# Turning the expert product as one tile and three, with the next rows' second half between them

## The chip, the cores and the metric

The kernel runs on one core of a Trainium2 chip. A core has TensorE (matmuls and transposes, PE in the profile, its weight loads PEld), VectorE (DVE), ScalarE (ACT), GpSimd (POOL), SyncE (SP) and DMA queues. The metric is the time of one execution on the device in microseconds (us); it is given as the median of several runs.

## What is computed

One inference step of a decoder trunk with one layer, on 1088 tokens (1024 of a prompt, 64 of samples) of width 1024, in float32. After the mixer come a router and a mixture of 16 experts, of which each token takes two. The change lies in the experts:

```python
hid = jax.nn.silu(jnp.einsum('nd,edf->nef', x, w_gate)) * jnp.einsum('nd,edf->nef', x, w_up)
hid = hid * combine[..., None].astype(hid.dtype)
y = jnp.einsum('nef,efd->nd', hid, w_down)
```

with d = 1024, f = 512 and e = 16 experts. A final RMSNorm follows.

## The kernel before

Five stages run one after another: input projection, attention, output projection with routing, experts, final norm. In the expert stage (`experts`, from L1752) the tokens of each expert are gathered into blocks of up to 128 rows. With these inputs there are 24 blocks for 16 experts: eight experts have one block, eight have two.

Every matmul is done in a split form: an operand is a rounded part (`_hi`) and a remainder (`_rest` or `_lo`), and three products are summed: hi x hi, hi x rest, lo x hi. ScalarE makes each `_hi` by a copy, VectorE each remainder by a subtraction. For the weights these are L1743 and L1748, each on half a matrix (128x2048) at a time, six of each for an expert; the split of the next expert's gate and up matrices is done during the first block of the present expert, that of its own down matrix at the start of that block. So a first block carries twelve of these long instructions on ScalarE and VectorE, and a second block none.

The order on each engine is written out by hand, and semaphores tie them together. For block b:

- TensorE: `project` gate (24 matmuls, L1972, L1973, L1976), then up; four transposes of the next block's rows (`turn_rows(0)`, L1964); four transposes of the product `hid` (L1997), two into `hturn[0]` and two into `hturn[1]`, each pair behind a wait for its part of `hid`; four more of the next rows (`turn_rows(1)`); then the down projection: 16 matmuls with `hidT_hi` as the loaded operand (L2006, L2007), tile by tile, of which tiles 0 and 2 wait for the copy of their pair, and 8 with `hidT_lo` (L2011).
- ScalarE: split of down and gate, `silu` of gate (L1890), splits, then the two copies `hidT_hi` (L1897), the two of the next rows `rowsT_hi` (L1878), a split, and half of `y_out` (L1906), which waits for this block's down projection and for the scatter of the block before to have landed.
- VectorE: splits, the product `hid` of up and silu in two parts (L1937), `hidT_lo` in two parts (L1940), each behind its copy on ScalarE, the next rows' `rowsT_lo` (L1924), splits, the other half of `y_out` (L1951), and the copy of gathered rows into `rows` (L1919).
- GpSimd: the scatter that adds `y_out` to the result (L1864) and the gather of the rows of block b + 3 (L1847). 
- SyncE: loads of the next weights, behind the end of an expert's gate, up and down products.

Of the kernel before, what the change touches and what calls it, by code (L numbers as in the profile page):

```python
# [20 lines left out]
F32 = mybir.dt.float32  # L21
# [4 lines left out]
ALU = mybir.AluOpType  # L26
# [3 lines left out]
P = 128  # L30
# [29 lines left out]
FT = FF // P  # L60
# [1691 lines left out]
def experts(nc, io, keep):  # L1752
# [5 lines left out]
    with ExitStack() as stack:  # L1758
        p = Pools(nc, stack)
# [39 lines left out]
        add_begun = p.sem("add_begun")  # L1799
        expert_begun = p.sem("expert_begun")  # L1800

        def expert_loops(eng, block_step):

            def one(pair, half, last):
                e = 2 * pair + half if pair is not FIRST or half else FIRST
                here = (pair, half)
                following = None if last else ((pair, 1) if half == 0 else (pair + 1, 0))
                first = eng.value_load(ends[0:1, bass.ds(e, 1)], min_val=0, max_val=MAXB - 1)
                after = eng.value_load(ends[0:1, bass.ds(e + 1, 1)], min_val=1, max_val=MAXB)
                block_step(FIRST if e is FIRST else first, here, following)  # L1810
                with eng.If(first + 1 < after):
                    with eng.Fori(first + 1, after) as b:
                        block_step(b)

            one(0, 0, False)
            one(0, 1, False)
            with eng.Fori(1, NE // 2 - 1) as pair:
                one(pair, 0, False)
                one(pair, 1, False)
            one(NE // 2 - 1, 0, False)  # L1820
            one(NE // 2 - 1, 1, True)
# [52 lines left out]
        @block.scalar  # L1874
        def _(act):
            def rows_hi(b, c):
                act.wait_ge(turned, 2 * b + c + 1)
                nc.scalar.activation(rowsT_hi[:, 4 * c:4 * c + 4, :], turn[c][:, :].rearrange("p (k c) -> p k c", k=4), ACT.Copy).then_inc(rowsT_hi_made, 1)  # L1878

            def block_step(b, here=None, following=None):  # L1880

                if here:
                    if b is not FIRST:
                        act.wait_ge(downed, b)
                    moe.split_hi(act, "down", *here, 0)
                    moe.split_hi(act, "down", *here, 1)
                if following:
                    moe.split_hi(act, "gate", *following, 0)
                act.wait_ge(gated, b + 1)
                nc.scalar.activation(silu[:, :], gate[:, :], ACT.Silu).then_inc(silued, 1)  # L1890
                if following:
                    moe.split_hi(act, "gate", *following, 1)
                    moe.split_hi(act, "up", *following, 0)

                for c in range(2):
                    act.wait_ge(hid_turned, 2 * b + c + 1)
                    nc.scalar.activation(hidT_hi[:, 2 * c:2 * c + 2, :], hturn[c][:, 0:2 * P].rearrange("p (k c) -> p k c", k=2),  # L1897
                                         ACT.Copy).then_inc(hidT_hi_made, 1)
                rows_hi(b + 1, 0)
                rows_hi(b + 1, 1)  # L1900
                if following:
                    moe.split_hi(act, "up", *following, 1)
                act.wait_ge(downed, b + 1)
                if b is not FIRST:
                    act.wait_ge(y_stored, 16 * b)
                nc.scalar.activation(y_out[:, 0:512], y[0][:, :], ACT.Copy, scale=slot_w[:, bass.ds(b, 1)]).then_inc(y_act, 1)  # L1906

            rows_hi(FIRST, 0)
            rows_hi(FIRST, 1)
            expert_loops(act, block_step)  # L1910

        @block.vector
        def _(dve):
            def fetch(b):

                if b is not FIRST:
                    dve.wait_ge(turned, 2 * b)
                dve.wait_ge(gathered, 16 * b + 16)
                nc.vector.tensor_copy(rows[:, :], landing[:, :]).then_inc(rows_ready, 1)  # L1919

            def rows_lo(b, c):
                dve.wait_ge(rowsT_hi_made, 2 * b + c + 1)
                hi = rowsT_hi[:, 4 * c:4 * c + 4, :]
                nc.vector.tensor_tensor(rowsT_lo[:, 4 * c:4 * c + 4, :], turn[c][:, :].rearrange("p (k c) -> p k c", k=4),  # L1924
                                        hi.bitcast(F32), ALU.subtract).then_inc(rowsT_lo_made, 1)

            def block_step(b, here=None, following=None):
                if here:
                    moe.split_rest(dve, "down", *here, 0)
                    moe.split_rest(dve, "down", *here, 1)  # L1930
                if following:
                    moe.split_rest(dve, "gate", *following, 0)
                dve.wait_ge(silued, b + 1)
                dve.wait_ge(upped, b + 1)
                for c in range(2):
                    cols = slice(2 * P * c, 2 * P * c + 2 * P)
                    nc.vector.tensor_tensor(hid[:, cols], up[:, cols], silu[:, cols], ALU.mult).then_inc(hid_ready, 1)  # L1937
                for c in range(2):
                    dve.wait_ge(hidT_hi_made, 2 * b + c + 1)
                    nc.vector.tensor_tensor(hidT_lo[:, 2 * c:2 * c + 2, :], hturn[c][:, 0:2 * P].rearrange("p (k c) -> p k c", k=2),  # L1940
                                            hidT_hi[:, 2 * c:2 * c + 2, :].bitcast(F32), ALU.subtract).then_inc(hidT_lo_made, 1)
                rows_lo(b + 1, 0)
                rows_lo(b + 1, 1)
                if following:
                    moe.split_rest(dve, "gate", *following, 1)
                    moe.split_rest(dve, "up", *following, 0)
                    moe.split_rest(dve, "up", *following, 1)
                dve.wait_ge(downed, b + 1)
                if b is not FIRST:
                    dve.wait_ge(y_stored, 16 * b)  # L1950
                nc.vector.tensor_scalar(y_out[:, 512:D], y[1][:, :], slot_w[:, bass.ds(b, 1)], None, ALU.mult).then_inc(y_dve, 1)  # L1951
                fetch(b + 2)

            fetch(FIRST)
            rows_lo(FIRST, 0)
            rows_lo(FIRST, 1)
            fetch(1)
            expert_loops(dve, block_step)

        @block.tensor  # L1960
        def _(pe):
# [20 lines left out]
            with pe.Fori(0, NE // 2) as pair:  # L1982
                for half in range(2):
# [5 lines left out]
                    with pe.Fori(first, after) as b:  # L1989
                        project(gate, b, moe.hi["gate"][half], moe.rest["gate"][half], done + 2).then_inc(gated, 1)  # L1990
                        project(up, b, moe.hi["up"][half], moe.rest["up"][half], done + 4).then_inc(upped, 1)
                        pe.wait_ge(rows_ready, b + 2)
                        turn_rows(0)
                        for c in range(2):
                            pe.wait_ge(hid_ready, 2 * b + c + 1)
                            for k in range(2):
                                ins = nc.tensor.transpose(hturn[c][:, P * k:P * k + P], hid[:, P * (2 * c + k):P * (2 * c + k + 1)], ident[:, :])  # L1997
                            ins.then_inc(hid_turned, 1)
                        turn_rows(1)
                        pe.wait_ge(moe.rest_made, done + 6)  # L2000
                        for k in range(FT):
                            if k % 2 == 0:
                                pe.wait_ge(hidT_hi_made, 2 * b + k // 2 + 1)
                            for j in range(2):
                                cols = slice(512 * j, 512 * j + 512)
                                nc.tensor.matmul(y[j][:, :], hidT_hi[:, k, :], moe.hi["down"][half][:, k, cols], start=(k == 0), stop=False)  # L2006
                                nc.tensor.matmul(y[j][:, :], hidT_hi[:, k, :], moe.rest["down"][half][:, k, cols], start=False, stop=False)  # L2007
                        pe.wait_ge(hidT_lo_made, 2 * b + 2)
                        for k in range(FT):
                            for j in range(2):  # L2010
                                ins = nc.tensor.matmul(y[j][:, :], hidT_lo[:, k, :], moe.hi["down"][half][:, k, 512 * j:512 * j + 512],  # L2011
                                                       start=False, stop=(k == FT - 1))
                        ins.then_inc(downed, 1)
# [181 lines left out]
```

## Time and profile before

| | |
|---|---|
| median of 3 runs | 1201.89 us (1200.39 to 1202.03) |
| the profiled execution | 1202.3 us, its span 1200.5 us |
| PE busy in the span | 1069.8 us (89%) |
| DVE busy | 587.9 us (49%) |
| ACT busy | 469.8 us (39%) |
| POOL busy | 145.3 us (12%) |
| mean granted clock of TensorE | 0.94 |

The shares are means over stages with different limits; what the change is worth is to be read in the expert stage, 710 to 1162 us. There TensorE is busy nearly all the time, and VectorE works through the whole of a first block. A row of the timeline merges alike instructions that follow each other: its second figure is the time from the start of the first to the end of the last, `x4` their number, and the bracket at its end is the idle time of that engine before them and who ended it.

### The profile page before, as it was taken

To read this page: it belongs to the slowest core of one execution; us is meant where nothing else is said; L and a number is where in the kernel's file an instruction comes from. 1 tells how busy PE (TensorE), PEld (TensorE's weight loads), DVE (VectorE), ACT (ScalarE), POOL (GpSimd) and SP (SyncE) were. 2 spreads that over 40 slices of the span, in tenths; PEclk is the share of its full clock that TensorE was granted. 3 is DMA by queue.
4 is the path that set the end of the run, shared out by engine and by line. 5 is a ranking of instruction groups with operands and counts; after the bars stand their busy time and mean duration, and the time that the engine had idled before them with its cause. 6 is when DMAs were issued, how large, how long until landed. Compare 5 with 4: busy or idle time off the path is not lost. (4 is left out here: it accounts for less than half of the span.)

```text
span 1200.5 us, 16318 instructions
## 1 busy us (share of the span) xinstructions
PE 1069.8 (89%) x5923; PEld 868.2 (72%) x5924; DVE 587.9 (49%) x972; ACT 469.8 (39%) x736; POOL 145.3 (12%) x133
## 2 busy tenths in 40 slices
PE   5799999999899998878999549999999999999960
PEld 3699999998556666546888337877877777778750
DVE  5411113420166653325335565664599966649534
ACT  5311111101366652224123223554378645547324
POOL 0000000000100000000000011312234342223420
PEclk8699999999899998988999759999999999999995
DMA  6125111222440007866322554578699965789438
GB/s 221 64 54 203 49 53 53 71 65 78 122 131 1 2 1 239 249 186 205 131 106 97 200 221 120 193 265 280 226 380 397 377 209 200 273 291 395 118 70 314
DMA packets 104161, 207.34 MB, mean 173 GB/s; under 512 B 12648, under 2 KB 47249, under 8 KB 104075
## 3 DMA queue, kind: packets, MB, share of 16 engines
q1 hardware_dynamic: 96764, 179.89, 42.0%
q0 software_dynamic: 7344, 26.74, 9.2%
q8 instruction: 33, 0.54, 0.2%
q14 instruction: 20, 0.16, 0.0%
HBM read 175.75 MB, written 36.55 MB: 177 GB/s over the span
## 5 line engine op out<-in xcount | busy, mean ns | idle before, releaser
L545 PE MATMUL bank<-xT_hi,w_hi 128*128 128x384 f32 (+1 forms) x432 | 96.2, 331 | 5.4 <-DVE w_rest L408 5.4
L545 PE MATMUL bank<-xT_rest,w_hi 128*128 128x384 f32 (+1 forms) x432 | 95.7, 330 | 0.0
L545 PE MATMUL bank<-xT_hi,w_rest 128*128 128x384 f32 (+1 forms) x432 | 94.5, 327 | 0.0
L1864 POOL DMA_INDIRECT x_rows<-y_out,out_id x24 | 64.7, 2694 | 212.1 <-DVE rows L1919 195.3
L1748 DVE TENSOR_TENSOR down_rest<-w_down,down_hi 128x2048 fp32r<-128x2048 f32 x32 | 71.9, 2288 | 20.3 <-ACT down_hi L1743 19.4
L545 PEld LDWEIGHTS bank<-xT_hi,w_hi 128*128 128x128 f32 x432 | 74.1, 190 | 5.6 <-issue 5.6
L1972 PE MATMUL gate<-gate_hi,rowsT_hi 128*128 128x512 f32 x192 | 77.2, 402 | 0.7 <-ACT rowsT_hi L1878 0.7
L1973 PE MATMUL gate<-gate_rest,rowsT_hi 128*128 128x512 f32 x192 | 77.7, 405 | 0.0
L2006 PE MATMUL y<-down_hi,hidT_hi 128*128 128x512 f32 x192 | 76.8, 400 | 0.0
L1973 PE MATMUL up<-up_rest,rowsT_hi 128*128 128x512 f32 x192 | 75.6, 394 | 0.0
L1972 PE MATMUL up<-up_hi,rowsT_hi 128*128 128x512 f32 x192 | 75.2, 392 | 0.0
L2007 PE MATMUL y<-down_rest,hidT_hi 128*128 128x512 f32 x192 | 74.8, 390 | 0.0
L545 PEld LDWEIGHTS bank<-xT_rest,w_hi 128*128 128x128 f32 x432 | 74.5, 191 | 0.0
L1748 DVE TENSOR_TENSOR gate_rest<-w_gate,gate_hi 128x2048 fp32r<-128x2048 f32 x32 | 73.1, 2284 | 2.5 <-ACT gate_hi L1743 2.5
L545 PEld LDWEIGHTS bank<-xT_hi,w_rest 128*128 128x128 f32 x432 | 73.3, 189 | 0.0
L1748 DVE TENSOR_TENSOR up_rest<-w_up,up_hi 128x2048 fp32r<-128x2048 f32 x32 | 71.8, 2285 | 0.0
L1743 ACT ACTIVATE down_hi<-w_down 128x2048 fp32r<-128x2048 f32 x32 | 59.7, 1914 | 13.9 <-issue 13.9
L1743 ACT ACTIVATE up_hi<-w_up 128x2048 fp32r<-128x2048 f32 x32 | 61.3, 1920 | 0.0
L1743 ACT ACTIVATE gate_hi<-w_gate 128x2048 fp32r<-128x2048 f32 x32 | 61.0, 1906 | 0.0
L937 ACT ACTIVATE logit<-logit,neg_max 128x256 f32<-128x256 f32 (+7 forms) x80 | 52.2, 656 | 5.1 <-DVE neg_max L1006 5.0
L1937 DVE TENSOR_TENSOR hid<-up,silu 128x256 f32<-128x256 f32 x48 | 18.1, 420 | 71.3 <-PE up L1976 71.3
L817 DVE COPY probsT<-turn 128x256 f32<-128x256 f32 (+4 forms) x60 | 28.6, 496 | 47.5 <-PE turn L1143 30.5
(278 smaller groups left out, 2087.2 us busy)
## 6 DMA issues: line engine op xcount, KB each, us to landing
w_gate<-in_w_gate SPq DMA_DIRECT2D x16, 2048.0 KB, 12.0
w_up<-in_w_up SPq DMA_DIRECT2D x16, 2048.0 KB, 11.9
w_down<-in_w_down SPq DMA_DIRECT2D x16, 2048.0 KB, 12.6
stage<-in_w_in SPq DMA_DIRECT2D x6, 1536.0 KB, 7.0
k_cache<-in_cache_b_k SPq DMA_DIRECT2D x8, 768.0 KB, 9.4
bias_scratch<-bias_one_row SPq DMA_DIRECT2D x1, 5800.0 KB
mixT<-in_x_prompt SPq DMA_DIRECT2D x8, 512.0 KB, 3.9
x<-in_x_prompt SPq DMA_DIRECT2D x8, 512.0 KB, 3.9
```

Source lines behind the costliest of these rows:

```text
L545: ins = nc.tensor.matmul(bank[3 * (n % 2) + i][:, 0:m], w_tiles(wt, n // CH)[:, k, cols], xt[:, k, c:c + m], start=(k == 0 and x == 0), st ...
L817: ins = nc.vector.tensor_copy(out, src)
L937: nc.scalar.activation(logit[:, u % 4, 0:n], logit[:, u % 4, 0:n], ACT.Exp, bias=neg_max[:, u:u + 1], scale=-1.0, accum_out=denom[:, u:u + ...
L1743: self.nc.scalar.activation(self.hi[which][half][:, k, :], self.raw[which][half][:, k, :], ACT.Copy).then_inc(self.hi_made, 1)
L1748: self.nc.vector.tensor_tensor(self.rest[which][half][:, k, :], self.raw[which][half][:, k, :], self.hi[which][half][:, k, :].bitcast(F32) ...
L1864: nc.gpsimd.indirect_dma_start(out=io["x1"], out_offset=bass.IndirectOffsetOnAxis(ap=out_id[:, :], axis=0), in_=y_out[:, :], in_offset=Non ...
L1937: nc.vector.tensor_tensor(hid[:, cols], up[:, cols], silu[:, cols], ALU.mult).then_inc(hid_ready, 1)
L1972: nc.tensor.matmul(out[:, :], rowsT_hi[:, k, :], hi[:, k, :], start=(k == 0), stop=False)
L1973: nc.tensor.matmul(out[:, :], rowsT_hi[:, k, :], rest[:, k, :], start=False, stop=False)
L2006: nc.tensor.matmul(y[j][:, :], hidT_hi[:, k, :], moe.hi["down"][half][:, k, cols], start=(k == 0), stop=False)
L2007: nc.tensor.matmul(y[j][:, :], hidT_hi[:, k, :], moe.rest["down"][half][:, k, cols], start=False, stop=False)
```

## The change

The product `hid` (512 columns, four tiles of 128) was handled in two parts of two tiles each. It is now handled in a part of one tile and a part of three, on all three engines: the product and the remainder on VectorE, the transposes on TensorE, the copy on ScalarE. The four transposes of the next rows' second half, which stood behind the transposes of both parts, now stand between those of the first and the second part. In the down projection tile 0 waits for the first copy as before, and tile 1 for the second; tile 2 no longer has a wait of its own. The buffers stay the same.

```diff
+        HID_PARTS = ((0, 1), (1, FT))
...
-                for c in range(2):
+                for c, (k0, k1) in enumerate(HID_PARTS):
                     act.wait_ge(hid_turned, 2 * b + c + 1)
-                    nc.scalar.activation(hidT_hi[:, 2 * c:2 * c + 2, :], hturn[c][:, 0:2 * P].rearrange("p (k c) -> p k c", k=2),
+                    nc.scalar.activation(hidT_hi[:, k0:k1, :], hturn[c][:, 0:(k1 - k0) * P].rearrange("p (k c) -> p k c", c=P),
                                          ACT.Copy).then_inc(hidT_hi_made, 1)
...
-                for c in range(2):
-                    cols = slice(2 * P * c, 2 * P * c + 2 * P)
+                for k0, k1 in HID_PARTS:
+                    cols = slice(P * k0, P * k1)
                     nc.vector.tensor_tensor(hid[:, cols], up[:, cols], silu[:, cols], ALU.mult).then_inc(hid_ready, 1)
-                for c in range(2):
+                for c, (k0, k1) in enumerate(HID_PARTS):
                     dve.wait_ge(hidT_hi_made, 2 * b + c + 1)
-                    nc.vector.tensor_tensor(hidT_lo[:, 2 * c:2 * c + 2, :], hturn[c][:, 0:2 * P].rearrange("p (k c) -> p k c", k=2),
-                                            hidT_hi[:, 2 * c:2 * c + 2, :].bitcast(F32), ALU.subtract).then_inc(hidT_lo_made, 1)
+                    nc.vector.tensor_tensor(hidT_lo[:, k0:k1, :], hturn[c][:, 0:(k1 - k0) * P].rearrange("p (k c) -> p k c", c=P),
+                                            hidT_hi[:, k0:k1, :].bitcast(F32), ALU.subtract).then_inc(hidT_lo_made, 1)
...
-                        for c in range(2):
+                        for c, (k0, k1) in enumerate(HID_PARTS):
                             pe.wait_ge(hid_ready, 2 * b + c + 1)
-                            for k in range(2):
-                                ins = nc.tensor.transpose(hturn[c][:, P * k:P * k + P], hid[:, P * (2 * c + k):P * (2 * c + k + 1)], ident[:, :])
+                            for k in range(k0, k1):
+                                ins = nc.tensor.transpose(hturn[c][:, P * (k - k0):P * (k - k0) + P], hid[:, P * k:P * k + P], ident[:, :])
                             ins.then_inc(hid_turned, 1)
-                        turn_rows(1)
+                            if c == 0:
+                                turn_rows(1)
                         pe.wait_ge(moe.rest_made, done + 6)
                         for k in range(FT):
-                            if k % 2 == 0:
-                                pe.wait_ge(hidT_hi_made, 2 * b + k // 2 + 1)
+                            if k < 2:
+                                pe.wait_ge(hidT_hi_made, 2 * b + k + 1)
```

## Rows read from the trace of the kernel before

**Rows 1.** The page: the span, and TensorE's busy time.

```profile
span 1200.5 us, 16318 instructions
PE 1069.8 (89%) x5923; PEld 868.2 (72%) x5924; DVE 587.9 (49%) x972; ACT 469.8 (39%) x736; POOL 145.3 (12%) x133
```

**Rows 2.** Busy time of each engine in the expert stage.

```profile
core 0: us, PE busy (x) PEld busy (x) DVE busy (x) ACT busy (x) POOL busy (x), PEclk, DMA share, GB/s
710.00:1162.00 452.00, 444.42 (x2024) 357.69 (x2023) 303.79 (x287) 240.35 (x239) 132.49 (x97) 0.99 0.73 251
```

**Rows 3.** Timeline of one block: start us, us, engine, line, operation [idle before].

```profile
781.84 0.76 DVE L1937 TENSOR_TENSOR hid<-up,silu 128x256 f32<-128x256 f32 x2 [7.09 <-PE up L1976]
782.32 0.53 PEld L1997 LDWEIGHTS hturn<-ident,hid 128*128 128x128 f32 x4 [0.39 <-DVE hid L1937]
...
782.80 0.72 ACT L1897 ACTIVATE hidT_hi<-hturn 128x256 fp32r<-128x256 f32 x2 [5.94 <-PE hturn L1997]
782.82 0.47 PEld L1964 LDWEIGHTS turn<-ident,rows 128*128 128x128 f32 x4
...
783.21 0.76 DVE L1940 TENSOR_TENSOR hidT_lo<-hturn,hidT_hi 128x256 fp32r<-128x256 f32 x2 [0.61 <-ACT hidT_hi L1897]
783.29 0.19 PEld L2006 LDWEIGHTS y<-down_hi,hidT_hi 128*128 128x128 f32 x1
...
783.41 1.08 ACT L1878 ACTIVATE rowsT_hi<-turn 128x512 fp32r<-128x512 f32 x2
...
784.09 0.19 PEld L2006 LDWEIGHTS y<-down_hi,hidT_hi 128*128 128x128 f32 x1
...
788.66 0.19 PEld L1972 LDWEIGHTS gate<-gate_hi,rowsT_hi 128*128 128x128 f32 x1
```

**Rows 4.** Waits of the expert stage: us in total, times, longest.

```profile
PEld hturn L1997 <- DVE hid L1937: 10.3, 24, 0.9
```

**Rows 5.** Groups by line and shape, 560 to 1190 us: busy, mean ns.

```profile
L1924 DVE TENSOR_TENSOR rowsT_lo<-turn,rowsT_hi 128x512 fp32r<-128x512 f32 x50 | 32.3, 687 | 3.5 <-ACT rowsT_hi L1878 2.0
...
L1878 ACT ACTIVATE rowsT_hi<-turn 128x512 fp32r<-128x512 f32 x50 | 27.2, 599 | 22.9 <-PE turn L1964 22.9
...
L1964 PEld LDWEIGHTS turn<-ident,rows 128*128 128x128 f32 x200 | 24.7, 144 | 13.2 <-DVE rows L1919 10.0
...
L1940 DVE TENSOR_TENSOR hidT_lo<-hturn,hidT_hi 128x256 fp32r<-128x256 f32 x48 | 18.2, 421 | 14.8 <-ACT hidT_hi L1897 14.8
L1937 DVE TENSOR_TENSOR hid<-up,silu 128x256 f32<-128x256 f32 x48 | 18.1, 420 | 71.3 <-PE up L1976 71.3
...
L1897 ACT ACTIVATE hidT_hi<-hturn 128x256 fp32r<-128x256 f32 x48 | 17.2, 384 | 66.8 <-PE hturn L1997 66.7
```

**Rows 6.** Timeline of VectorE through three experts of one block each.

```profile
874.24 0.76 DVE L1937 TENSOR_TENSOR hid<-up,silu 128x256 f32<-128x256 f32 x2 [0.60 <-PE up L1976]
...
877.64 2.28 DVE L1748 TENSOR_TENSOR gate_rest<-w_gate,gate_hi 128x2048 fp32r<-128x2048 f32 x1
...
889.91 2.29 DVE L1748 TENSOR_TENSOR gate_rest<-w_gate,gate_hi 128x2048 fp32r<-128x2048 f32 x1
892.68 0.76 DVE L1937 TENSOR_TENSOR hid<-up,silu 128x256 f32<-128x256 f32 x2 [0.48 <-PE up L1976]
...
905.07 4.50 DVE L1748 TENSOR_TENSOR down_rest<-w_down,down_hi 128x2048 fp32r<-128x2048 f32 x2 [1.05 <-ACT down_hi L1743]
...
911.69 0.75 DVE L1937 TENSOR_TENSOR hid<-up,silu 128x256 f32<-128x256 f32 x2
```

**Rows 7.** Timeline of GpSimd: two scatters behind a busy VectorE, one free.

```profile
885.91 7.76 POOL L1864 DMA_INDIRECT x_rows<-y_out,out_id  x1 [11.53 <-DVE rows L1919]
...
904.33 1.59 POOL L1864 DMA_INDIRECT x_rows<-y_out,out_id  x1 [1.53 <-DVE rows L1919]
...
1090.31 3.35 POOL L1864 DMA_INDIRECT x_rows<-y_out,out_id  x1 [11.57 <-DVE rows L1919]
```

**Rows 8.** Timeline of ScalarE: y_out in two following blocks.

```profile
881.66 0.69 ACT L1906 ACTIVATE y_out<-y,slot_w 128x512 f32<-128x512 f32 x1 [2.94 <-PE y L2011]
...
901.03 0.69 ACT L1906 ACTIVATE y_out<-y,slot_w 128x512 f32<-128x512 f32 x1 [3.90 <-DMA x_rows<-y_out,out_id]
```

## The prediction

> **What bounds the kernel now.** I read the page's engine shares first, then the stretches of the expert stage, then one block in order of time, and last the queues of VectorE, GpSimd and ScalarE through the stage. The profiled execution took 1202.3 us around a span of 1200.5 us [rows 1], so 1.8 us lie outside the span. The change touches only the 24 blocks of rows in the expert stage, 710 to 1162 us. There TensorE is busy 444.4 of 452.0 us at a granted clock of 0.99 [rows 2]; nothing but its own queue, and what its queue waits for, can move the time. So a gain has to shorten TensorE's gaps, and a loss has to come from an engine that makes TensorE wait.
>
> One block in order of time [rows 3] shows the place. Let t be the start of the first hid product (781.84 us). TensorE has finished the up projection and turned the first half of the next rows, and its weight loader waits 0.39 us for the product: the first load of L1997 is at t+0.48, 0.06 us behind the product's end (t+0.417). In the whole stage this wait is 10.3 us, once in each of 24 blocks [rows 4]. Then come eight transposes, four of hid and four of the next rows, and the first load of the down projection at t+1.45. Eight transposes thus take 0.97 us. The last four, which wait for nothing, take 0.47 us, a load of 0.14 us and three steps of 0.11 us; at 0.11 us a step, eight are 0.88 us, so about 0.09 us inside is the wait of the third transpose for the second product, which ends at t+0.76.
>
> **The change, part by part.** No instruction is added or removed: 12 transposes, two products, two copies on ScalarE, two subtractions on VectorE in each block, cut 128 and 384 columns in place of 256 and 256. Durations for the new widths are not in the trace; I take straight lines through its rows [rows 5]. ScalarE: 256 columns 0.384, 512 columns 0.599 us, so 0.84 ns a column: 128 columns about 0.28, 384 about 0.49. VectorE with a PSUM source: 256 columns 0.421, 512 columns 0.687 us, 1.04 ns a column: 128 about 0.28, 384 about 0.55. The bounds are an operation that costs as much as one of 256 columns (0.42 and 0.38), and one at half of it (0.21 and 0.19).
>
> *Product.* The first part ends at t+0.28 in place of t+0.42; the second still ends at t+0.76, since the two sum to the same columns.
>
> *Transposes.* The first hid transpose can be loaded at t+0.28+0.06 = t+0.34, 0.14 us earlier. Next come the four of the rows' second half, which have been ready for a block, so TensorE now works while VectorE makes the second product. They end their steps at t+0.34+5x0.11 = t+0.89, after t+0.82, when the 384 columns are seen. The inner wait is gone. The down projection's first load can come at t+0.34+8x0.11 = t+1.22, and allowing the 0.03 us by which it came late before, t+1.25. Its own wait is for ScalarE's copy of one tile: transposed by about t+0.67, copied from t+0.71 to t+0.99; it hides. Gain so far 1.45-1.25 = 0.20 us a block.
>
> *The new short wait.* Tile 1 of the down projection now needs the copy of three tiles. Its load is the fifth, 0.80 us after the first (783.29 to 784.09) [rows 3], so it is due at t+2.05. The last hid transpose starts streaming at about t+1.23; before, the copy began 0.3 us behind the start of the transpose that it waited for, so it now runs from t+1.54 to t+2.03 and is seen 0.06 us later, t+2.09. That is 0.04 us late; bounds 0 to 0.1. **Gain a block on TensorE: 0.20-0.04 = 0.16 us**, bounds 0.05 (a narrow product costs as much as a wide one, so that only the inner wait goes) and 0.20. If all 24 blocks had it, 3.8 us.
>
> *What becomes late.* VectorE subtracts the three tiles only after that copy, and ScalarE's two copies of the next rows stand behind it. These began at t+1.57 and begin now at about t+1.94: **0.37 us later**, and all that stands behind them on VectorE is later by as much: two rowsT_lo, gate_rest, two up_rest, y_out, the copy of the next rows, and the scatter that GpSimd issues after y_out. Who waits for these? The next gate projection wants gate_rest; in the block from 874.24 it starts at t+3.40 and takes 2.28, ending at t+5.68, now t+6.05, and TensorE turns to gate at t+6.82-0.16 [rows 3, 6]. Covered. The next product waits for VectorE itself. In eight second blocks of an expert it idled about 7.1 us before the product (781.84) [rows 3], and in first blocks behind them down_rest waits for ScalarE and TensorE, which move together. Covered. There remain seven blocks in which one expert of one block follows another directly: those from 892.68, 911.69, 930.20, 949.22, 967.74, 1097.08 and 1115.58 us (the first two stand in [rows 6]). VectorE is busy there through all of the block: its idle time before the product is 0.48 to 0.57 us in five, and nothing in two. Back-to-back instructions start 0.08 us before the end of the one before, so the slack is 0.56 us; the change takes 0.37 us by delay and 0.16 us by TensorE's shorter block, 0.53 us. Three hundredths remain: TensorE still sets these five.
>
> *The two blocks that lose.* The products at 911.69 and 949.22 come 0.57 us late (19.01 us after the one before, 18.44 in the block ahead of it). The chain [rows 6 to 8]: the scatter begun at 885.91 stays on GpSimd for 7.76 us and ends 1.47 us behind VectorE's gate_rest (889.91+2.29); it has landed at 901.0; ScalarE's y_out, which waits for that, starts at 901.03 in place of about 900.1; down_hi, down_rest (905.07, 1.05 us of waiting) and the product follow. Its origin is the end of gate_rest, now 0.37 us later. So from the product at 874.24 to that at 911.69, 37.45 us, comes 37.82 us, a loss of 0.37 us where two blocks at 0.16 would have gained. The same holds from 911.69 to 949.22. These pairs hold four of the 24 blocks.
>
> A row and a page bear on this scatter. GpSimd's same instruction takes 1.6 us when VectorE rests, 7.76 us four times when it starts behind a down_rest, and once only 3.35 us, ending 1.5 us behind the first boundary between two VectorE instructions (1090.31) [rows 7]. The Trainium skill (SBUF — State Buffer, the section "SBUF: two separate sides") says that the port pair shared by VectorE and GpSimd is locked for a whole instruction, also by a VectorE operation with two SBUF inputs, and goes to whoever starts first. By that rule the hid product, with one operand in PSUM, keeps GpSimd out no longer, and the sum stands as above; and any boundary may let the scatter in, which is the second rival below.
>
> **Sum.** 20 blocks x 0.16 = 3.2 us gained, 2 x 0.37 = 0.74 lost: 2.5 us. The profiled execution of 1202.3 would become 1199.8; it lies 0.4 us above the median of 1201.89, so the median becomes **1199.4 us**. No DMA is issued elsewhere; SyncE's weight loads stand behind gated, upped and downed and come with TensorE.
>
> **Rivals.** I count as told from no change what is more than 0.2%, 2.4 us, away.
> *Nothing to be had*: narrow operations cost nearly what wide ones do, or the wait for the three-tile copy takes back what the earlier start gives. At 0.05 us a block, 20x0.05-0.74 = 0.3 us: 1201.6. For it speaks that both estimates are of widths that no row shows, and that the copy is due within hundredths of its use; against it two straight lines from four rows.
> *The scatter gets in early*: at the first boundary in the two long chains, as at 1090.31. Their late products vanish, 1.1 us, and all blocks gain: 24x0.16+1.1 = 4.9 us, 1197.0. For it one case in five.
> *The scatter comes later still*: if it needs VectorE idle and not only a boundary, it waits past the product (0.76 us more), since the idle time before it is used up; each pair loses 1.1 in place of 0.37: 3.2-2.2 = 1.0 us gained, 1200.9. If besides the one at 1090.31 misses its boundary, its landing falls behind y_out of the next block, one more late product of about 1.1 us: no gain, 1201.9.
> *Slower*: the wait for the three-tile copy stands on TensorE's queue ahead of 20 matmuls of each block, with nothing to run in its place. It decides once it is more than 0.20 us: from there each 0.1 us more costs 2.4 us. At 0.35 us a block, a loss of 24x0.15+0.74 = 4.3 us: 1206.2. It needs a copy of 384 columns to be seen 0.31 us later than I have it. Against it: 512 columns take 0.60 us, only 0.11 above my 0.49.
>
> **How the numbers follow.** My sum 0.42; scatter early 0.14; nothing to be had 0.18; scatter later 0.16; slower 0.10. My own case lies on both sides of the 0.2% line (0.20 or 0.12 us a block give 3.3 or 1.7 us): two thirds of it is faster, 0.28; with 0.14 of the early scatter and some of the others 0.04, faster is 0.46. Slower is 0.10. The rest, 0.44, is within 0.2%; the single likeliest value is just beyond the line. Range: from the early scatter (1197.0) to no gain (1201.9), widened slightly below for 0.20 us a block: 1196.6 to 1202.0; outside stand the slower case and a little below.
>
> **What the profile after would show.** Right: the first L1997 load at t+0.34, the four L1964 loads between, the first L2006 load near t+1.25, ScalarE's wide copy at about 0.49 us, and rowsT_lo 0.37 us later. Between products 18.27 us in place of 18.43 in blocks behind an idle VectorE; 19.5 us for the two late ones. Wrong: a L2006 load of tile 1 that waits over 0.1 us for ScalarE; VectorE without idle time and TensorE waiting over 0.4 us for its product in the seven blocks; scatters of 7.76 us where there were short ones.

## The result, and the profile after

The changed kernel takes 1194.62 us (median of 6 runs, 1192.54 to 1196.65), the kernel before beside it 1201.94 us (1198.49 to 1203.64): a ratio of 0.9943, with a 95% interval of 0.9925 to 0.9962. It is faster by 7.3 us between the medians and by 6.9 by the ratio, whose interval is 4.6 to 9.0. I had given 1199.4 us, 2.5 us faster than the median shown, with a range of 1196.6 to 1202.0. The direction was right, the size about a third of the truth, and the median lies 2.0 us below the range.

The profiled execution took 1193.65 us. Its page begins:

```profile
span 1191.9 us, 16318 instructions
PE 1062.5 (89%) x5923; PEld 864.3 (73%) x5924; DVE 588.1 (49%) x972; ACT 470.9 (40%) x736; POOL 136.7 (11%) x133
```

The number of instructions is that of [rows 1]. The line numbers of the expert stage have moved by three or more (L1937 is now L1940, L1997 is L2000, L2006 is L2010). Busy time in the expert stage, to set beside [rows 2]:

```profile
core 0: us, PE busy (x) PEld busy (x) DVE busy (x) ACT busy (x) POOL busy (x), PEclk, DMA share, GB/s
710.00:1155.00 445.00, 437.99 (x2014) 354.90 (x2012) 302.68 (x285) 239.53 (x237) 124.34 (x97) 0.99 0.73 254
```

The granted clock is the same 0.99, the higher of TensorE's two levels (2.4 GHz) nearly throughout. One block in order of time, the fourth, as in [rows 3]:

```profile
777.07 0.76 DVE L1940 TENSOR_TENSOR hid<-up,silu 128x128 f32<-128x128 f32 x2 [6.53 <-PE up L1979]
777.41 0.14 PEld L2000 LDWEIGHTS hturn<-ident,hid 128*128 128x128 f32 x1 [0.25 <-DVE hid L1940]
777.47 0.47 PEld L1967 LDWEIGHTS turn<-ident,rows 128*128 128x128 f32 x4
777.78 0.28 ACT L1900 ACTIVATE hidT_hi<-hturn 128x128 fp32r<-128x128 f32 x1 [5.70 <-PE hturn L2000]
777.91 0.36 PEld L2000 LDWEIGHTS hturn<-ident,hid 128*128 128x128 f32 x3
778.24 0.19 PEld L2010 LDWEIGHTS y<-down_hi,hidT_hi 128*128 128x128 f32 x1
...
778.54 0.49 ACT L1900 ACTIVATE hidT_hi<-hturn 128x384 fp32r<-128x384 f32 x1 [0.49 <-PE hturn L2000]
778.81 0.19 PEld L2011 LDWEIGHTS y<-down_rest,hidT_hi 128*128 128x128 f32 x1
778.93 1.08 ACT L1881 ACTIVATE rowsT_hi<-turn 128x512 fp32r<-128x512 f32 x2
779.09 0.19 PEld L2010 LDWEIGHTS y<-down_hi,hidT_hi 128*128 128x128 f32 x1
779.27 0.19 PEld L2011 LDWEIGHTS y<-down_rest,hidT_hi 128*128 128x128 f32 x1
...
783.63 0.19 PEld L1975 LDWEIGHTS gate<-gate_hi,rowsT_hi 128*128 128x128 f32 x1
```

Count from t = 777.07. The first hid transpose is loaded at t+0.34, and the first load of the down projection is at t+1.17, where it was at t+1.45. The load that needs the second copy (779.09) comes 0.28 us behind the one before it in place of 0.23, so it waited 0.05 us. The next follows after 0.18: from the first load of the down projection to the sixth it is 1.03 us, and in the profile of before (783.29 to 784.32) it is 1.03 us too, one step of 0.11 and four of 0.23. The next block's gate starts at t+6.56, where it was at t+6.82. **So a block is 0.26 us shorter**, and the short new wait costs nearly nothing. There are 24 blocks: 6.2 us.

The widths that no row before had, by shape:

```profile
L1943 DVE TENSOR_TENSOR hidT_lo<-hturn,hidT_hi 128x384 fp32r<-128x384 f32 x24 | 13.4, 558 | 16.2 <-ACT hidT_hi L1900 16.2
L1940 DVE TENSOR_TENSOR hid<-up,silu 128x384 f32<-128x384 f32 x24 | 13.1, 548 | 0.0
...
L1900 ACT ACTIVATE hidT_hi<-hturn 128x384 fp32r<-128x384 f32 x24 | 11.8, 492 | 11.5 <-PE hturn L2000 11.5
L1943 DVE TENSOR_TENSOR hidT_lo<-hturn,hidT_hi 128x128 fp32r<-128x128 f32 x24 | 7.0, 292 | 6.6 <-ACT hidT_hi L1900 6.6
L1940 DVE TENSOR_TENSOR hid<-up,silu 128x128 f32<-128x128 f32 x24 | 7.0, 291 | 64.3 <-PE up L1979 64.3
L1900 ACT ACTIVATE hidT_hi<-hturn 128x128 fp32r<-128x128 f32 x24 | 6.6, 276 | 60.4 <-PE hturn L2000 60.4
```

Each is within 0.01 us of the straight lines of the prediction (0.28, 0.55, 0.49).

The chain of one-block experts, first VectorE, then GpSimd, then ScalarE, as in [rows 6 to 8]:

```profile
868.16 0.76 DVE L1940 TENSOR_TENSOR hid<-up,silu 128x128 f32<-128x128 f32 x2 [0.60 <-PE up L1979]
...
884.12 2.29 DVE L1748 TENSOR_TENSOR gate_rest<-w_gate,gate_hi 128x2048 fp32r<-128x2048 f32 x1
886.33 0.76 DVE L1940 TENSOR_TENSOR hid<-up,silu 128x128 f32<-128x128 f32 x2
...
898.99 4.49 DVE L1748 TENSOR_TENSOR down_rest<-w_down,down_hi 128x2048 fp32r<-128x2048 f32 x2 [1.02 <-ACT down_hi L1743]
...
905.60 0.75 DVE L1940 TENSOR_TENSOR hid<-up,silu 128x128 f32<-128x128 f32 x2
```

```profile
880.12 7.76 POOL L1867 DMA_INDIRECT x_rows<-y_out,out_id  x1 [11.84 <-DVE rows L1922]
```

```profile
895.04 0.69 ACT L1909 ACTIVATE y_out<-y,slot_w 128x512 f32<-128x512 f32 x1 [3.96 <-DMA x_rows<-y_out,out_id]
```

VectorE's idle time before the product at 886.33 is gone, and the product after it is late, 19.27 us behind: the mechanism of the prediction. But the two intervals sum to 37.44 us, as in [rows 6] (37.45), where I had 37.82. The late interval is itself longer than before (19.27 and not 19.01), while the ordinary one is shorter (18.17 and not 18.44), so the pair has gained nothing over the late pair of before. In this execution three products were late (905.60, 943.02 and 1107.41; the third by only 0.6 us), in the profile of before two.

The stage from the first to the last product took 421.5 us after and 426.1 us before, 4.6 us less, with one more late product. The rest of the difference between the two profiles lies ahead of the experts: the first product starts at 722.48 us and not at 726.46. Nothing in that part was changed, and this is what the controls below are for.

### The profile page after: what moved, and what is told of

Read it like the earlier page. It is cut to its first block and busy times, and to the rows that moved or that the text cites. A ratio compares the mean times of both kernels' runs of the same rounds, so it can differ in the third digit from the quotient of the medians.

```text
span 1191.9 us, 16318 instructions
## 1 busy us (share of the span) xinstructions
PE 1062.5 (89%) x5923; PEld 864.3 (73%) x5924; DVE 588.1 (49%) x972; ACT 470.9 (40%) x736; POOL 136.7 (11%) x133
## 5 line engine op out<-in xcount | busy, mean ns | idle before, releaser
L545 PE MATMUL bank<-xT_hi,w_hi 128*128 128x384 f32 (+1 forms) x432 | 95.4, 329 | 5.4 <-DVE w_rest L408 5.4
L545 PE MATMUL bank<-xT_rest,w_hi 128*128 128x384 f32 (+1 forms) x432 | 94.4, 327 | 0.0
L1867 POOL DMA_INDIRECT x_rows<-y_out,out_id x24 | 58.5, 2437 | 188.1 <-DVE rows L1922 171.1
L2010 PE MATMUL y<-down_hi,hidT_hi 128*128 128x512 f32 x192 | 77.0, 401 | 0.0
L1640 PE MATMUL y<-w_out_hi,mix_hi 128*128 128x512 f32 (+1 forms) x144 | 46.2, 402 | 5.3 <-DVE w_rest L1499 5.3
```

The costliest lines, as they stand in the source:

```text
L545: ins = nc.tensor.matmul(bank[3 * (n % 2) + i][:, 0:m], w_tiles(wt, n // CH)[:, k, cols], xt[:, k, c:c + m], start=(k == 0 and x == 0), st ...
L1640: ins = nc.tensor.matmul(y[t % 2][j][0:n, :], rows[:, t % 2, k, 0:n], wt[:, k, 512 * j:512 * j + 512], start=(k == 0 and x == 0), stop=(k ...
L1867: nc.gpsimd.indirect_dma_start(out=io["x1"], out_offset=bass.IndirectOffsetOnAxis(ap=out_id[:, :], axis=0), in_=y_out[:, :], in_offset=Non ...
```

## The experiments

**The order alone.** Two parts of two tiles as before, but the rows' second half is turned between them.

```diff
-        HID_PARTS = ((0, 1), (1, FT))
+        HID_PARTS = ((0, 2), (2, FT))
...
-                            if k < 2:
-                                pe.wait_ge(hidT_hi_made, 2 * b + k + 1)
+                            if k % 2 == 0:
+                                pe.wait_ge(hidT_hi_made, 2 * b + k // 2 + 1)
```

Expected:

> The order alone: the product keeps its two parts of two tiles, the next rows' second half is turned between them. Let t be the start of the first product. Theory A (the two edits need each other): the first pair of hid transposes is still loaded at t+0.48, and the down projection's first load cannot come before the copy of two tiles, made at t+1.34, is seen, so it comes at t+1.41 to t+1.45, a gain of 0 to 0.04 us a block; all 24 blocks give 0 to 1 us, within 0.3 us of no change if the three late products grow as before: ratio 0.999 to 1.001. Theory B (what was gained is the inner wait for the second product, which the four rows' transposes cover): 0.1 us a block or more, 2.6 us, ratio 0.998 or less, first load at t+1.34 or earlier.

Measured: 1196.71 us (12 runs) against 1199.47 (29 runs), ratio 0.998, interval 0.9968 to 0.9993. Its timeline (first product at 798.51):

```profile
798.99 0.20 PEld L2000 LDWEIGHTS hturn<-ident,hid 128*128 128x128 f32 x2 [0.39 <-DVE hid L1940]
799.16 0.47 PEld L1967 LDWEIGHTS turn<-ident,rows 128*128 128x128 f32 x4
799.46 0.38 ACT L1900 ACTIVATE hidT_hi<-hturn 128x256 fp32r<-128x256 f32 x1 [0.85 <-PE hturn L2000]
799.59 0.25 PEld L2000 LDWEIGHTS hturn<-ident,hid 128*128 128x128 f32 x2
799.96 0.19 PEld L2010 LDWEIGHTS y<-down_hi,hidT_hi 128*128 128x128 f32 x1
```

The down projection's first load is at t+1.45 again. TensorE is through its transposes 0.1 us sooner, and waits for the copy of two tiles, which ends at 799.84 (799.46+0.38). Intervals between products are 18.42 and 18.50 us, and from the first product to the last it is 425.1 us (control: 425.3). By the trace the order alone gives nothing in the expert stage, as theory A has it. The ratio says 2.4 us faster (0.8 to 3.8), the size that theory B gave. But the sign of B in the trace, a first load at t+1.34 or earlier, is not there, the control's own ratio is 0.9989, and the two intervals overlap. So I go by the trace for the mechanism; where the 2.4 us of the times come from is not shown. The profiled execution, 1199.22 us, was the second slowest of the twelve.

**The split alone.** One tile and three, the rows' second half behind both.

```diff
-                            if c == 0:
-                                turn_rows(1)
+                        turn_rows(1)
```

Expected:

> The split alone: parts of one and three tiles, the next rows' second half turned behind both. Theory A: the first hid transpose is loaded at t+0.34, but the second has nothing ahead of it and waits for the second product to t+0.82; three hid and four rows' transposes at 0.11 us follow and the down projection's first load comes at t+1.5 to t+1.6, 0.05 to 0.15 us later than before: 1 to 4 us slower over 24 blocks, ratio 1.001 to 1.003. Theory C (the earlier first transpose and the earlier first copy carry the gain by themselves): first load at t+1.3 or earlier, 3 us faster or more, ratio 0.9975 or less.

Measured: 1201.7 us (12 runs), ratio 1.0018, interval 1.0007 to 1.003: slower. Its timeline (first product at 798.02):

```profile
798.37 0.14 PEld L2000 LDWEIGHTS hturn<-ident,hid 128*128 128x128 f32 x1 [0.25 <-DVE hid L1940]
798.74 0.28 ACT L1900 ACTIVATE hidT_hi<-hturn 128x128 fp32r<-128x128 f32 x1 [0.61 <-PE hturn L2000]
798.83 0.31 PEld L2000 LDWEIGHTS hturn<-ident,hid 128*128 128x128 f32 x3 [0.33 <-DVE hid L1940]
799.11 0.47 PEld L1967 LDWEIGHTS turn<-ident,rows 128*128 128x128 f32 x4
799.55 0.19 PEld L2009 LDWEIGHTS y<-down_hi,hidT_hi 128*128 128x128 f32 x1
```

The first transpose is loaded at t+0.35, 0.13 us earlier than before, and the second waits 0.33 us for the second product; the down projection starts at t+1.53, as theory A has it. From the first product to the last it is 427.5 us (control: 425.3). So in the expert stage each edit by itself is worth nothing or less: the narrow first part makes the copy early enough, and the rows' transposes fill the time until the wide part comes.

**Controls: the kernels themselves again.** The kernel before three times more and the changed one twice more, with no edit. Expected, in the order in which they ran (the last two are single executions, each with a profile and one time):

> The kernel before, unchanged, as a control of what the measurement and the stages ahead of the experts do. Theory N (the 4 us by which the changed kernel reached the experts earlier in its profile is spread between executions): this kernel's own first product starts anywhere between 722 and 727 us after the span's start, and the ratio is within 0.002 of 1. Theory S (a shift that belongs to the changed program): it starts within 1 us of 726.5 again, as in the profile of before.

> The changed kernel again. In the expert stage, from the first product to the last, 421.5 us again (within 1 us, by how many scatters get in early). Theory N: the whole ratio lies near what the expert stage alone gives, 4.6 of 1202 us, 0.9962, and the first product starts anywhere between 722 and 727 us. Theory S: it starts within 1 us of 722.5, and the ratio stays near 0.9943 or below.

> The changed kernel for the third time, on the chip of the other three. First product to last 419.3 us plus 0.5 to 1.1 us for each late product, of which there are none to four; ratio to before 0.994 to 0.9955. If its start of the expert stage, 722.5 us twice, belongs to the program, it is within 1 us of that; if it is spread between executions, it may lie anywhere from 722 to 727.

> The kernel before again, one look at where it reaches the experts. It started them at 726.5 and 725.9 us, the changed kernel at 722.5, 722.6 and 723.3. Theory N (spread between executions, by TensorE's granted clock in the attention of the samples): in this look or the next the start is 724 us or earlier. Theory S (it belongs to the program): 725.5 to 727 both times.

> As the run before it: a start of the experts at 724 us or earlier for theory N, 725.5 to 727 for theory S; stage from first to last product 425.3 us plus 0.6 for each late one.

Measured, with the two profiles already told (late: products more than 0.5 us behind their turn; start: the first product; stage: first product to last; clock: granted from 455 to 545 us):

| | start, us | clock | late | stage, us | ratio to before |
|---|---|---|---|---|---|
| before, first profile | 726.5 | 0.91 | 2 | 426.1 | |
| before again | 725.9 | 0.91 | 0 | 425.3 | 0.9989 (0.9976 to 1.0003) |
| before, single execution | 723.5 | 0.94 | 0 | 425.8 | |
| before, second one | 727.4 | 0.92 | 0 | 425.8 | |
| after, first profile | 722.5 | 0.93 | 3 | 421.5 | 0.9943 (0.9925 to 0.9962) |
| after again | 722.6 | 0.93 | 1 | 419.3 | 0.9944 (0.9926 to 0.9963) |
| after, third | 723.3 | 0.94 | 1 | 419.8 | 0.9935 (0.9917 to 0.9954) |

By their ratios the three comparisons give 6.9, 6.7 and 7.8 us, by their medians 7.3, 7.6 and 7.4. The stage gives 6.0 us between "again" and "again", and 5.5 us between the means of all profiles. The start of the kernel before is spread over 4 us, as theory N has it, so the first pair of profiles, 8.6 us apart, showed too much. The spread arises ahead of the experts, where nothing was changed, and much of it in one stretch: from the last transpose of L1143 (about 451 us) to the first `mix_hi` of L1452 (about 544 us) it is 94.4, 95.4, 92.0 and 93.0 us in the four profiles of before, in the order of the table, and 92.0 us in each of the three after; the two longest lie at a granted clock of 0.91, the four of 92.0 us at 0.93 or 0.94. "Before again" and "after" reach L1143's last transpose at the same 450.2 us. Against N stands that all three starts of the changed kernel lie at the low end, as theory S has it; those of the six variants of this section lie between 722.3 and 724.7 us. What is left over the 6.0 us of the stage, 0.7 to 1.8 us by the ratios, is inside the intervals and may be chance or a shift that belongs to the program. That stays open. The profile of "before again" was the slowest of its twelve executions (1201.68 us, their median 1199.14), so its late start is not the usual one.

The lateness is no fixed property of a kernel: three profiles of the kernel before have no late product and one has two, and the changed kernel has one to three. But a scatter of 7.76 us costs the changed kernel more, as VectorE's slack is used up. In the second single execution of the kernel before one begins at 1090.71, and the product after it comes 18.64 us behind the one ahead, where it is 18.50 to 18.63 us without one there. At the same place the changed kernel has 18.81 us with it, in two profiles, and 18.22 without. The profile of before has scatters of 7.76 us, and "before again" has none there:

```profile
885.65 3.35 POOL L1864 DMA_INDIRECT x_rows<-y_out,out_id  x1 [11.58 <-DVE rows L1919]
904.06 3.35 POOL L1864 DMA_INDIRECT x_rows<-y_out,out_id  x1 [5.93 <-DVE rows L1919]
922.57 3.35 POOL L1864 DMA_INDIRECT x_rows<-y_out,out_id  x1 [5.94 <-DVE rows L1919]
```

In all these profiles a scatter of 3.35 us and one of 7.76 us start alike, 0.39 to 0.41 us into a down_rest, so the moment of the start does not tell them apart.

**How much slack VectorE has left.** The changed kernel with a useless copy in each block (the result stays the same).

```diff
                 rows_lo(b + 1, 1)
+                nc.vector.tensor_copy(spare[:, :], hturn[0][:, 0:PROBE])
```

with PROBE = 128 and a tile `spare` for it. Expected:

> The changed kernel with a useless copy of 128 columns from PSUM on VectorE in each block, behind rowsT_lo: about 0.21 us more of VectorE's time a block; what is computed stays the same. Theory V (in the seven one-block experts the change has used up VectorE's slack, 0.03 us or less is left): each of their intervals grows from 18.17 or 18.25 us to 18.3 to 18.45, the others stay at 18.17 and 18.25, and the stage from first to last product is about 1.3 us longer than 419.3 (late products apart). Rival (TensorE still has the lead by more than that): no interval changes.

Measured in a single execution, 1193.73 us. Two of the seven intervals in its timeline:

```profile
868.91 0.75 DVE L1942 TENSOR_TENSOR hid<-up,silu 128x128 f32<-128x128 f32 x2 [0.61 <-PE up L1982]
872.61 0.28 DVE L1949 COPY spare<-hturn 128x128 f32<-128x128 f32 x1
...
887.27 0.75 DVE L1942 TENSOR_TENSOR hid<-up,silu 128x128 f32<-128x128 f32 x2
...
905.62 0.75 DVE L1942 TENSOR_TENSOR hid<-up,silu 128x128 f32<-128x128 f32 x2
```

Six of the seven intervals before a one-block expert's product are 18.35 or 18.36 us and one, a late one, is 19.19; without the copy they were 18.15 to 18.25 in the changed kernel, late ones apart. Of the other sixteen, fourteen stay at 18.14 to 18.26, one is 18.31 and one 18.54, which I can't account for. The added work of 0.2 us lengthens those blocks by 0.1 to 0.2 us, as theory V has it: the change has brought VectorE level with TensorE there. A variant with three such copies, expected at 18.7 to 18.85 us, gave no time, so how the blocks grow from there is not shown.

**ScalarE's half of y_out put later**, so that the landing of a scatter no longer holds up the weights' split.

```diff
                     moe.split_hi(act, "down", *here, 1)
+                if state["held"]:
+                    y_half(b - 1, b)
...
-                act.wait_ge(downed, b + 1)
-                if b is not FIRST:
-                    act.wait_ge(y_stored, 16 * b)
+                if here and type(here[0]) is int and here == (0, 1):
+                    state["held"] = True
+                if not state["held"]:
+                    y_half(b, b + 1)
```

`y_half` holds the old wait for the down projection and the copy; GpSimd passes the landing of each scatter on through the counter `add_begun`. Expected:

> The changed kernel with ScalarE's half of y_out moved behind the two halves of the next block's down split, so that a late landing of a scatter no longer holds up down_hi, down_rest and the next product. Theory L (the late products come from that chain alone): no product is late any more, whatever the scatters take (some of 7.76 us may stay); all blocks are 18.1 to 18.3 us apart, first product to last 418.5 to 419.5 us; 0 to 2.5 us faster than the changed kernel, as many products as it has late in an execution: ratio to before 0.992 to 0.9945. Rival D (VectorE's own queue has no slack left in the seven one-block experts, and the late ones come from that): blocks of 19 us stay.

Measured: 1193.28 us (6 runs), ratio 0.9949, interval 0.993 to 0.9968, outside the ratio expected and no better than the changed kernel beside it (0.9935). The profile has one late product, behind a scatter of 7.64 us:

```profile
1086.27 0.75 DVE L1953 TENSOR_TENSOR hid<-up,silu 128x128 f32<-128x128 f32 x2
...
1098.45 4.49 DVE L1748 TENSOR_TENSOR down_rest<-w_down,down_hi 128x2048 fp32r<-128x2048 f32 x2 [0.55 <-issue]
...
1105.06 0.75 DVE L1953 TENSOR_TENSOR hid<-up,silu 128x128 f32<-128x128 f32 x2
```

It comes 18.79 us after the one before, late by 0.6 us. At this same place the changed kernel has a late product in two of its three profiles, and both times it comes 18.81 us after the one before it and its down_rest has waited 0.56 us, there for ScalarE:

```profile
1100.80 4.49 DVE L1748 TENSOR_TENSOR down_rest<-w_down,down_hi 128x2048 fp32r<-128x2048 f32 x2 [0.56 <-ACT down_hi L1743]
```

So here the edit gained nothing. ScalarE's down_hi is on time now (its first half starts at 1093.22), and still down_rest waits 0.55 us, for nothing that the trace shows as a semaphore. VectorE's own half of y_out waits for the same landing (GpSimd saw it at 1095.09), and the queue behind it starts from there; that this is the 0.6 us is argued, not shown. Theory L, that ScalarE's chain alone makes the late products, does not hold: at this place VectorE is as late without it. Whether ScalarE's part counts where a product is late by 1.0 to 1.1 us (905.60 and 943.02) this profile can't show, since none was late there.

**Three parts of one, one and two tiles**, with two of the rows' four transposes ahead of the first hid transpose.

```diff
-        HID_PARTS = ((0, 1), (1, FT))
+        HID_PARTS = ((0, 1), (1, 2), (2, FT))
+        hbank = (hturn[0], gate, hturn[1])
...
                         turn_rows(0)
+                        turn_rows(1, 0, 2)
...
                             if c == 0:
-                                turn_rows(1)
+                                turn_rows(1, 2, 4)
```

The waits for the parts count in threes, and the down projection waits at tiles 0, 1 and 2.

Expected, and for both edits together:

> The changed kernel with three parts of one, one and two tiles (the second transposed into the bank of gate), and two of the four transposes of the next rows' second half put ahead of the first hid transpose. Theory G (the 0.25 us for which TensorE still waits for the first product can be filled, and the two-tile copy comes sooner): first load of the down projection at t+1.11 in place of t+1.17, ScalarE's rowsT_hi at t+1.7 in place of t+1.86, blocks of 18.11 us where there were 18.17: 1.4 us faster than the changed kernel, ratio to before 0.9935 or less. Rival: the product's last part is seen later with one more instruction in front of it, which takes it back: t+1.15 or later, and VectorE is 0.1 us or more busier a block: no change or slower than the changed kernel.

> Both: three parts and the late half of y_out. If the two are independent, their gains add: 1.4 us and up to 2.5 us below the changed kernel, first product to last 417 to 418 us, ratio to before 0.991 to 0.9935. If VectorE's queue binds, its seven one-block experts stay above 18.2 us and the three parts give less than 1 us.

Measured: 1192.03 us, ratio 0.9943 (0.9921 to 0.9965) where 0.9935 or less was expected, and with the late half of y_out 1191.38 us, ratio 0.9931 (0.9912 to 0.9949), where the changed kernel beside them had 1192.18. The times don't separate the three. The trace does (three parts, first product at 796.20):

```profile
795.70 0.80 PEld L1968 LDWEIGHTS turn<-ident,rows 128*128 128x128 f32 x6
...
796.55 0.14 PEld L2003 LDWEIGHTS hturn<-ident,hid 128*128 128x128 f32 x1
...
797.31 0.19 PEld L2013 LDWEIGHTS y<-down_hi,hidT_hi 128*128 128x128 f32 x1
```

The wait for the first product is gone, the down projection starts at t+1.11, and blocks are 18.08 and 18.16 us apart. From first product to last it is 417.2 us, 2.1 us below the changed kernel ("again", with its one product late by 0.6 us), though one interval is 18.48 us. No product is late, and with the late half of y_out none is either, at 417.4 us: the two gains don't add, and the late half shows none. Its one-block experts are 18.08 to 18.18 us apart, so VectorE's queue does not hold them above 18.2. In the interval of 18.48 us ScalarE waits for a load of weights, in a stretch (941 to 959 us) in which the 16 DMA engines are busy throughout (share 1.04, 383 GB/s):

```profile
958.57 1.92 ACT L1743 ACTIVATE up_hi<-w_up 128x2048 fp32r<-128x2048 f32 x1 [0.96 <-DMA w_up<-in_w_up]
```

## Why the prediction was wrong, by its own steps

*The place and the mechanism were right.* The first load of L2000 is at t+0.34 as written, the four L1967 loads stand behind it, the wide copy takes 0.49 us, and the wait for the second product is gone. Each of the two edits alone gives nothing in the expert stage, which the two first experiments show; the prediction had not asked it.

*The term that failed is the gain of a block, 0.16 us; it measures 0.26.* Two parts of it were too small. The first load of the down projection was put at t+1.25 and is at t+1.17. I counted eight steps of 0.11 us and added 0.03 us of lateness taken from before. In fact the step from a transpose that had waited to the one behind it is 0.06 us (777.41 to 777.47), and no lateness is left: 0.06 us and seven steps of 0.11 are the 0.83 us from t+0.34 to t+1.17. The lateness had a cause that goes away: in the order-alone run the load is held at t+1.45 by the copy of two tiles, so at least the end of my 0.97 us before was that copy's wait and not TensorE's pace. The inner wait of the third transpose was misread with it: it started at t+0.81 in place of t+0.65, 0.16 us late and not 0.09, and a second step of 0.06 us behind it hid a part. And the wait of tile 1 was put at 0.04 us lost; the load waits 0.05 us, but the next step makes it up, and of the 0.28 us by which the down projection starts sooner 0.26 are left at the end of the block. Over 24 blocks 0.10 us is 2.4 us, about half of what was missing. My bounds for the block, 0.05 to 0.20 us, did not hold it either: they came from the durations, and all of these were right, while the error sat in the steps between them.

*The second failure is that four blocks were written off.* I took the two late products of one profile for a fixture of the kernel and let them lose 0.37 us each in pairs, 0.74 us in all, and gave those four blocks no gain. The further profiles show none in the kernel before, three times, and three, one and one in the changed kernel: whether a scatter gets in at the first boundary between two VectorE instructions changes from one execution to the next. Taken over blocks that are not late, all 24 gain; that is 24x0.26 = 6.2 us, where 2.5 us were forecast. In the pair that could be compared (874.24 and 868.16) the loss was nil and not 0.37 us, because VectorE's delay was 0.30 us and not 0.37, and the scatter landed 0.2 us sooner behind its issue. That such a pair gains nothing was right in kind: its sum is 37.44 us, and 37.53 in the third profile of the changed kernel, against 36.4 for two ordinary blocks there.

*VectorE's slack* came out nearly as forecast: it is all but used up (0.03 us were to be left), and the added copy of 0.2 us shows at once in the seven blocks. But this was partly luck: the delay was smaller than forecast (0.30 us, not 0.37) and the block's gain larger (0.26, not 0.16), and their sum, 0.56 us in place of 0.53, is the whole slack.

*Rivals.* "The scatter gets in early" had the right direction, and its sum of 4.9 us was short for the same term of 0.16 us; the changed kernel's own profiles still have late products. The slower case and "nothing to be had" are out. "The scatter comes later still" is out too: at 880.12 it ended 1.47 us behind gate_rest with no idle time there. The Trainium skill (SBUF — State Buffer, "SBUF: two separate sides") gives the shared port pair for a whole instruction to whichever of the two starts first, while the other blocks. The trace agrees in so far as the scatters of 3.35 and 7.76 us end about 1.5 us behind the end of a VectorE instruction; no run here shows why a scatter takes the first boundary one time and the third another.

*Between 6.2 and the 7.3 us measured* lie 1.1 us that the stage does not explain. The intervals of the three comparisons reach down to 4.6, 4.4 and 5.5 us, so it need not be real.

## What to carry to other kernels

When an engine waits for another, its work after the wait is worth more than its count of steps says: read the pace from a stretch that waits for nothing at either end, and ask of every gap whose wait it is. Before a rare stall is made a term of the sum, look whether a second profile of the same kernel has it. And a split that lets one engine start sooner pays only together with work that fills the time until the larger part arrives: here either edit alone was worth nothing in the stage that it touches.

## What the runs showed of the hardware

A weight load that follows a transpose which had to wait starts 0.06 us behind it, where the steady step is 0.11 us. The same scatter instruction of GpSimd takes 1.6 us beside an idle VectorE, and 3.35 or 7.76 us when it starts 0.4 us into a subtraction of two SBUF tiles on VectorE, in executions of one and the same program. In the changed kernel a 7.76 us one made the product behind it 0.6 to 1.1 us late where a block of a one-block expert followed another. VectorE's 128-column operation at 0.29 us and ScalarE's at 0.28 lie on the straight line through wider ones.
